# Order of work between the last mLSTM head and the GLA output: two slabs, one early tile, two groups of small products

## The reference

```
mq, mk, mv, mo, mi, mf, gq, gk, gv, gg, glr = split(h @ w_in)
hm = rms_norm(mlstm(mq, mk, mv, mi, mf)) * sigmoid(mo)
log_a = log_sigmoid(glr @ w_gate_up + b_gate) / 16
hg, s = gla(gq / 8, gk, gv, log_a, s0)          # s = exp(log_a) s + k v ; o = q s
hg = rms_norm(hg) * silu(gg)
y += concat(hm, hg) @ w_out
```

## Time and profile before

| | us |
|---|---|
| median of 3 runs | 1421.3 |
| lowest, highest | 1418.34, 1423.42 |
| profiled execution | 1421.89 |
| its span | 1420.3 |
| TensorE busy in the span | 1371.3 |
| VectorE, ScalarE, GpSimd busy | 848.0, 527.8, 110.6 |

### The profile page before, as it was taken

One profiled execution on the slowest core, in us unless ns is written; L12 is line 12 of the kernel. 1 busy time (PEld: TensorE's weight loads), 2 busy tenths in 40 slices (PEclk: granted clock), 3 DMA queues, 4 the chain that ended last, 5 costly groups with the idle time before them and its releaser, 6 DMA issues.

```text
span 1420.3 us, 28954 instructions
## 1 busy us (share of the span) xinstructions
PE 1371.3 (97%) x11466; PEld 1314.0 (93%) x11466; DVE 848.0 (60%) x1284; ACT 527.8 (37%) x860; POOL 110.6 (8%) x158
## 2 busy tenths in 40 slices
PE   7999999989999999999999999997999999999997
PEld 7899998889999999999998778875999999999997
DVE  7565558856666666432364888887456666664221
ACT  5434445534332223322234565563432233222110
POOL 0221113111000000000001010000200000000000
PEclk9999998999999999999999999997999999999999
DMA  6566544122222223322127778772222222233320
GB/s 223 129 143 136 102 170 106 63 73 87 95 89 89 90 98 108 107 81 96 60 93 221 243 225 277 239 214 83 93 87 95 97 89 89 89 107 112 117 76 22
DMA packets 47369, 170.86 MB, mean 120 GB/s; under 512 B 6382, under 2 KB 7710, under 8 KB 47306
## 3 DMA queue, kind: packets, MB, share of 16 engines
q1 hardware_dynamic: 38938, 143.61, 29.7%
q0 software_dynamic: 8368, 26.38, 9.2%
HBM read 158.45 MB, written 11.51 MB: 120 GB/s over the span
## 4 chain that ended last, share of the span: by engine, by line
PE 88%; DVE 5%; issue 2%; ACT 2%; DMA 1%; POOL 0%; SPq 0%; DVEq 0%; ACTq 0%; POOLq 0%
PE ps L539 57%; PE ps L590 16%; PE ps L722 2%; PE ps L947 1%; PE ps L962 1%; PE ps L977 1%; PE ps L911 1%; PE ps L950 1%; PE ps L956 1%; DMA qb<-q_rows 1%; PE ps L1080 1%; DVE w_lo L1697 1%; ACT w_hi L1193 1%; DVE s_prod L2262 1%; PE ps L684 0%
## 5 line engine op out<-in xcount | busy, mean ns | idle before, releaser
L1697 DVE TENSOR_TENSOR w_lo<-raw,w_hi 128x1024 fp32r<-128x1024 f32 (+1 forms) x189 | 244.4, 1293 | 351.3 <-ACT w_hi L1193 351.3
L539 PE MATMUL ps<-h_hi,w_hi 128*128 128x260 f32 x1536 | 434.6, 283 | 0.8 <-DVE h_lo L1730 0.7
L539 PE MATMUL ps<-h_hi,w_lo 128*128 128x260 f32 x1536 | 434.0, 283 | 0.0
L539 PE MATMUL ps<-h_lo,w_hi 128*128 128x260 f32 x1536 | 432.4, 282 | 0.0
L1193 ACT CAST w_hi<-raw 128x1024 fp32r<-128x1024 f32 (+1 forms) x189 | 208.2, 1101 | 229.5 <-PE ps L539 223.3
L539 PEld LDWEIGHTS ps<-h_hi,w_hi 128*128 128x128 f32 x1536 | 289.0, 188 | 1.8 <-DVE h_lo L1730 1.1
L539 PEld LDWEIGHTS ps<-h_hi,w_lo 128*128 128x128 f32 x1536 | 288.8, 188 | 0.0
L539 PEld LDWEIGHTS ps<-h_lo,w_hi 128*128 128x128 f32 x1536 | 288.8, 188 | 0.1
L539 PE MATMUL ps<-a_lo,w_hi 128*128 128x260 f32 x704 | 199.0, 283 | 0.0
L539 PE MATMUL ps<-a_hi,w_hi 128*128 128x260 f32 x704 | 198.7, 282 | 0.0
L539 PE MATMUL ps<-a_hi,w_lo 128*128 128x260 f32 x704 | 198.7, 282 | 0.0
(11 more groups left out here) (399 smaller groups left out, 2178.5 us busy)
## 6 DMA issues: line engine op xcount, KB each, us to landing
raw<-in_w_ffn SPq DMA_DIRECT2D x88, 512.0 KB, 3.6
raw<-in_w_down SPq DMA_DIRECT2D x32, 704.0 KB, 4.1
k_pages<-in_cache_k SPq DMA_DIRECT2D x32, 512.0 KB, 5.4
v_pages<-in_cache_v SPq DMA_DIRECT2D x32, 512.0 KB, 7.2
raw<-in_w_rec_in SPq DMA_DIRECT2D x29, 512.0 KB, 6.5
raw<-in_w_att_kv SPq DMA_DIRECT2D x24, 512.0 KB, 5.4
raw<-in_w_rec_out SPq DMA_DIRECT2D x8, 512.0 KB, 3.7
raw<-in_w_att_q SPq DMA_DIRECT2D x8, 512.0 KB, 3.7
```

What stands on the lines that cost most here:

```text
L539: ins = TE.matmul(half(bank, h), w_part[:, buf, w], m_part[:, k_at + k, h * HALF:(h + 1) * HALF], start=start, stop=stop)
L1697: V.tensor_tensor(w_lo[:, n % 2, 0:nk * P], raw[:, n % RAW, 0:nk * P], w_hi[:, n % 2, 0:nk * P].bitcast(F32), ALU.subtract).then_inc(lo_sp ...
```

## The change

Four things. (1) The last head's slabs are 20, 21, 22, 23, 26, 27, and the queries and keys come one and two heads earlier. Its part 4 is no longer multiplied within the head but behind `decay_up(1)`, and the drain of it and the splits of output slab 0 move behind it: on ScalarE before the cast of `h_hi`, on VectorE behind the near factors. Two of the four output-gate tiles get their silu later, with its own loads of the function table. (2) Early tile 1 is multiplied between the near and the far products of pair 0. (3) The far products are grouped by shape, with the two halves of the partitions (`hh`) in turn, and the samples' products take the halves in turn. (4) At the end of the stage head 0's mix of pair 1 comes before early tile 7 is added, its high part before a weight split, both lows before that split, and the first late products of tile 1 before those of tile 0.

```diff
-HEAD_SLABS = [[13, 1, 5, 9, 24, 25], [14, 2, 6, 10, 26, 27], [15, 3, 7, 11, 16, 17], [18, 19, 20, 21, 22, 23]]
+HEAD_SLABS = [[13, 1, 5, 9, 24, 25], [14, 2, 6, 10, 16, 17], [15, 3, 7, 11, 18, 19], [20, 21, 22, 23, 26, 27]]
# TensorE
-                part(4)
+                if h < M_HEADS - 1:
+                    part(4)
...
             decay_up(1)
-            pe.wait_ge(drained, S_REC_IN - 1)
-            slab_part(S_REC_IN - 1, (S_REC_IN - 1) % 2, range(KT // 2), 2).then_inc(early_free, 1)
+            pe.wait_ge(drained, S_REC_IN - 2)
+            slab_part(S_REC_IN - 2, (S_REC_IN - 2) % 2, range(KT), 2)
             wait(pe, lD, "z0")
             wait(pe, lA, "abs0")
             v_chunks(0)
+            pe.wait_ge(drained, S_REC_IN - 1)
+            slab_part(S_REC_IN - 1, (S_REC_IN - 1) % 2, range(KT // 2), 2).then_inc(early_free, 1)
             slab_part(S_REC_IN - 1, (S_REC_IN - 1) % 2, range(KT // 2, KT), 2)
...
-            early(1, 2, 5)
...
                 near_levels(p, (4, 5), 5)
+                if p == 0:
+                    early(1, 2, 5)
...
-                for hh in range(2):
-                    r = slice(64 * hh, 64 * hh + 64)
-                    for b in range(B):
+                for b in range(B):
+                    for hh in range(2):
+                        r = slice(64 * hh, 64 * hh + 64)
...
+            wait(pe, oA, "rms1", 1)
+            wait(pe, oD, "lo1", 0)
+            late(1, range(2))
             wait(pe, rD, "m7")
-            wait(pe, oD, "lo1", 0)
             late(0, range(2))
-            wait(pe, oA, "rms1", 1)
-            late(1, range(2))
# ScalarE
-                    S.activation(z[:, 24:28, :], z[:, 24:28, :], ACT.Silu)
+                    S.activation(z[:, 24:26, :], z[:, 24:26, :], ACT.Silu)
...
-                rec_step(first + 4)
+                if h < M_HEADS - 1:
+                    rec_step(first + 4)
...
             own_decay(0)
+            rec_step(S_REC_IN - 2)
             act.wait_ge(early_free, 1)
...
             far_decays(0)
+            act.wait_ge(drained, S_REC_IN)
+            S.activation(z[:, 26:28, :], z[:, 26:28, :], ACT.Silu)
+            S.preload_act_table_set(LN_EXP)
             far_scores(0)
...
+            output_highs(1, (0,))
             split("rec_out", 0, 5, KT)
-            output_highs(1)
+            output_highs(1, (1,))
# VectorE
-                rec_split(4)
+                if h < M_HEADS - 1:
+                    rec_split(4)
...
             factors(0, "near", 2, len(LEVELS))
+            split("rec_out", 0, 0, KT)
...
+            mixes(1, (0,))
             early_drain(7, 0)
-            mixes(1)
+            mixes(1, (1,))
+            lows(1)
             split("rec_out", 0, 5, KT)
-            lows(1)
```

More of the change, by code:

```diff
@@ L788, in within @@
                 for c in range(NC_G):
+                    at_ = c * LC_G
                     for hh in range(2):
                         r = slice(64 * hh, 64 * hh + 64)
-                        at_ = c * LC_G
                         TE.matmul(ps[0:64, hh, at_ + 64:at_ + 128], lev[r, 0, at_:at_ + 64], lev[r, 0, at_ + 64:at_ + 128],
                                   start=True, stop=True)
-                        for b_ in (0, 64):
-                            s_, t_ = at_ + b_, at_ + b_ + BLK
+                for c in range(NC_G):
+                    at_ = c * LC_G
+                    for b_ in (0, 64):
+                        s_, t_ = at_ + b_, at_ + b_ + BLK
+                        for hh in range(2):
+                            r = slice(64 * hh, 64 * hh + 64)
                             ins = TE.matmul(ps[b_:b_ + BLK, hh, t_:t_ + BLK], lev[r, 1, s_:s_ + BLK], lev[r, 1, t_:t_ + BLK],
@@ L1454, in roots, with output_highs @@
                     rsqrt(two(sq[:, hh, :]), pair(bank), P, oA, f"lr{hh}", p).then_inc(oA.sem, 1)
-            def output_highs(p):
-                for hh in range(2):
+            def output_highs(p, heads=(0, 1)):
+                for hh in heads:
                     wait(act, oD, f"mix{hh}", p)
@@ L2117, in sample_states, with mixes @@
                 V.tensor_tensor(g_ss[:, :, :], g_ss[:, :, :], g_kv[:, :, :], ALU.add).then_inc(gD.sem, 1)
-            def mixes(p):
-                for hh, bank in ((0, 7), (1, 2)):
+            def mixes(p, heads=(0, 1)):
+                for hh in heads:
+                    bank = (7, 2)[hh]
                     wait(dve, oA, f"rms{hh}", p)
```

## The result

| | before | after |
|---|---|---|
| median (5 runs of each) | 1422.74 | 1429.81 |
| lowest, highest | 1418.34, 1426.57 | 1429.07, 1430.47 |
| profiled execution | 1421.89 | 1429.81 |
| its span | 1420.3 | 1428.2 |
| mean granted clock of TensorE | 0.984 | 0.980 |

The ratio is 1.0046, with a 95% interval from 1.003 to 1.0063: 6.5 us slower, between 4.3 and 9.0. The forecast was 1426.5, +5.0. Both holes are there, at nearly the predicted length, and most of the rest of the walk holds too. What was sized wrong is the clock behind the holes.

A forecast was written before the change was run, and what follows sets the result against it. TensorE, busy 97% of the span, was taken as the bound. Terms: -1.4 us at full clock, +6.8 for four clock falls, -0.4 hidden by VectorE, together +5.0; forecast 1426.5 us, range 1423 to 1430 (8 in 10: 1419.5 to 1433.5).

The forecast's parts named there:

- the walk: Step-by-step timing of the changed stage on TensorE, ScalarE and VectorE, summing to -1.4 us at full clock.
- First hole: At 213.84 us TensorE, without the moved slab, waits for ScalarE's square until 218.9: 5.0 us idle.
- Second hole: TensorE idles from 233.5 to 239.5, 6.0 us, until VectorE's split lets early tile 0 start, 11.0 us late.
- Regained up to early tile 2: From early tile 0 to early tile 2, the delay against before shrinks from 11.0 to 4.7 us at full clock.
- the lateness: Delay against the kernel before: 11.0 us at early tile 0, 4.7 at early tile 2.
- From there to the end: From early tile 2 to the stage's end at full clock: 3.6 - 1.0 - 1.7 - 2.3 = -1.4 us.
- The last low stretch: Half-clock stretch of 3.4 us at 293.2 in before, expected gone from the last samples: -1.7 us.
- the fourth fall: Drop to half clock late in pair 1 or at its samples, booked at 1.7 us.
- The clock: Four falls of TensorE's clock at 1.7 us each, 6.8 us, about 0.4 hidden by VectorE; the term trusted least.
- the shortest stretch shown is 3.4 us: Basis for pricing each clock fall: half of that length in dense products, 1.7 us; bounds 0 and 5.2.
- the clock stays down: Rival: half clock lasts through the small products, one or two 10.3 us stretches; 1430 to 1434 us, chance 0.14.
- the regrouping does nothing: Rival: far products stay at 3.4 us in pair 0 (+2.3), samples +1.0; 1429.8 us, chance 0.08.

The follow-up runs named there:

- Fill_both: The kernel after, with 40 products, overwritten and never read, put in each of TensorE's two holes: median 1428.35 us, ratio 1.0041.
- slabs_back: The kernel after, with part 1 (moved slabs, drain, splits and silu) undone: median 1416.80 us, ratio 0.9974 to before.
- samp_only: The kernel before, with only the samples' products taking the two halves in turn: median 1418.96 us, ratio 0.9975.
- end_only: The kernel before, with part 4 alone, the new order at the end of the stage: median 1418.40 us, ratio 0.9975.
- lows_late: The kernel before with parts 3 and 4, and VectorE's low parts of pair 0 moved behind pair 1's near blends: median 1413.79 us, ratio 0.9938.
- far_only: The kernel before, with only the far products regrouped: median 1420.29 us, ratio 0.9992.
- small_only: The kernel before, with part 3 alone (far products regrouped, samples' products alternating halves): median 1417.35 us, ratio 0.9964.
- small_end: The kernel before, with parts 3 and 4: median 1414.23 us, ratio 0.9943.
- early_front: The kernel after, with part 2 undone (early tile 1 ahead of the near blocks again): median 1426.57 us, ratio 1.0027 to before.

## Why the prediction was right, and what was sized wrong

**First hole.** Predicted 5.0 us, measured 5.07, released by the square as said.

**Second hole.** Predicted 6.0, measured 6.02. The chain behind the half slab, 8.9 us from the slab's half to early tile 0 (230.6 to 239.5), took 8.9 (235.78 to 244.66). Fill_both, where the clock stays up, starts early tile 0 at 239.70.

**Regained up to early tile 2.** At full clock the lateness was to be 4.7 us. Measured, with the 0.6 us at entry taken off, it is 11.8 (260.65 - 248.28 - 0.6). Of this 4.6 us are the clock in the first stretch (from the square to the end of the half slab 16.2 us, 219.53 to 235.78, for the 11.7 walked; the slab alone 8.29 for 5.85) and 2.3 the clock on early tile 0 (5.20 for 2.9). There remain 4.9. The far products took 1.07 (1.1 predicted), the waits for `g_kd` and the first blend 1.13 and 1.30 (about 1 each).

**From there to the end.** Predicted: from 4.7 to -1.4 and two more falls (3.4 less 0.4), together -3.1. Measured: from 11.8 to 8.6, -3.2. The sum is right by a balance of items that were not. The last low stretch did not go (303.5 to 307.0), so its 1.7 us were not won. Against this, the fourth fall (290.2) cost 0.6 us instead of 1.7 (lateness 12.5 at early tile 6, 13.1 at the samples, both with the 0.6 at entry), the samples of pair 1 gave 1.4 instead of 1.0, and the end waits 2.5 instead of 2.3. The 1.0 was a slip in part: 32 records at 78 ns are 2.5 us, not 2.4.

**The clock.** This is the mis-sized term. Four falls of 1.7 us were booked. There are five stretches, one of them already owed by the kernel before. The number was right; the length of the first two was not: 4.6 and 2.3 us of loss instead of 1.7 each, 3.5 us too little. 5.0 + 3.5 = 8.5, and the stage lost 8.6. So it is partly luck that the forecast of +5.0 lies as near the measured +6.5 as it does: some of the loss in the stage came back elsewhere. The step of the sum that failed is "the shortest stretch shown is 3.4 us": the first stretch lasted 13.5, of which 5.1 were dense products of a slab after 4 us of `sq` and `decay_up` at half clock. The upper bound stated, 5.2 for one stretch, was nearer for this one. The rival "the clock stays down" described this but put it at the small products and not at the slab. The time alone would not have told these apart: 1429.8 is also what the rival "the regrouping does nothing" gave, and 1430 where the clock stays down began. The far products at 1.07 us rule out the first.

**What the sum did not show.** It was a sum over the change as a whole. Its parts have both signs: part 1 +10 to +13, part 2 +2.7 to +4.4, samples -3.6, far -1.1, part 4 -3.6. With middle values, 11.5 + 3.5 - 3.6 - 1.1 - 3.6 = 6.7, against 6.5; this is no independent test, since two of the prices are differences from after itself. Part 2's price stood in the prediction as two waits for VectorE, and was not read as a price of that edit.

**Left open.** The stall without a releaser, 2.9 us in the earlier trace rows. I booked it as gone, as it was. In all eight kernels with the slab inside the head it is there in pair 0 (before 2.9, slabs_back 3.1, samp_only 2.8, end_only 3.0, lows_late 4.5, and less in far_only 1.2, small_only 1.8, small_end 1.9); with the slab moved it is at most 0.8 (early_front 0.5, fill_both 0.8, none in the other four). In the eight traces with the slab in the head a packet of the queue that carries instructions begins at 236.5 to 238.7 us, inside the stalls or up to 3 us ahead of one; in after one begins at 233.4, in dense products 5 us ahead of the second hole, and the next at 251.3, behind which nothing stalls. That the products run out of instructions is thus suggested, not shown; no run changed only that.

## What to carry to other kernels

Work that fills a wait of TensorE is worth more than the wait: here 5 us of idleness cost another 4.6 us behind it, in products at half clock. Before moving a block out of such a place, price the idleness and then the products behind it at half speed, and take for this the whole range of stretches on record, not only the shortest: the record before gave 1.7 to 5.2 us a stretch, and the two holes cost 4.6 and 2.3. A block that goes between two groups of small products also brings its drain along, which stands in another engine's list ahead of what these groups wait for; and where edits of both signs come in one change, timing them singly found a kernel 1% faster than the change as it was.

## What was not expected of the hardware

- After 5.07 us of idleness TensorE stood at 1.2 GHz (granted clock 0.50) for another 9.2 us of uninterrupted products, 219.5 to 228.7. After the second hole of 6.02 us it was 4.5 us (244.7 to 249.2). The clock fell at 215.2, 0.7 us into the first wait, and at 242.5, 3.9 us into the second.
- A product of one column: 32 records took 3.39 us with the halves one after the other and 1.95 us in turn, 61 ns a record. The prediction drew from the Trainium skill (TensorEngine Tiling (Array Packing), Instruction Overhead), where a free dimension of 1 takes as long as one of 60, that such products gain nothing. The trace does not agree with that conclusion, and the measurement decides. No run here compares the two widths, so the page's figure itself is not tested, and what the turn-taking hides is not shown.
- The times of one and the same kernel follow its mean granted clock: of 23 runs of before, the five at 0.981 and 0.982 took 1424.4 to 1426.2 us, the five at 0.986 and 0.987 took 1418.1 to 1420.6. A single run of each kernel could show 8 us either way.
